# Gated recurrence on one core: a unit's opening moves from VectorE to ScalarE, and GpSimd's low terms are cut into six parts

## What is computed

```python
def hgrn2_chunk_scan(q, k, v, log_f):
    """Chunkwise S_t = diag(f_t) S_{t-1} + k_t v_t^T, o_t = S_t^T q_t, scanned in token order."""
    def step(state, inp):
        qb, kb, vb, fb = inp
        b = jnp.cumsum(fb, axis=2)
        diff = b[:, :, :, None, :] - b[:, :, None, :, :]
        decay = jnp.exp(jnp.where(scan_order[:, :, None], diff, -jnp.inf))
        scores = jnp.einsum('bhtd,bhtsd,bhsd->bhts', qb, decay, kb)
        o = jnp.einsum('bhts,bhse->bhte', scores, vb) + jnp.einsum('bhtd,bhde->bhte', qb * jnp.exp(b), state)
        b_last = b[..., -1]
        state = jnp.exp(b_last[:, :, 0, :, None]) * state + jnp.einsum('bhsd,bhse->bhde', kb * jnp.exp(b_last - b), vb)
        return state, o
```

## Time and profile before

| | us |
|---|---|
| median of 3 runs | 3597.81 |
| lowest, highest | 3596.05, 3600.88 |
| the profiled execution, whole | 3596.66 |
| its span, first to last instruction | 3594.8 |
| `stage_hgrn` in it, from the first sigmoid to the last `take` | 1984.8 to 2188.8 |

### The profile page before, as it was taken

The page is one execution under the profiler, slowest core; times in us unless marked ns, Lnnn a source line. Parts: engine busy times, 40 slices in busy tenths (PEclk is TensorE's granted clock), DMA queues, the critical chain, the costliest instruction groups (busy, mean ns, idle before and its releaser), DMA issues. The chain is left out here.

```text
span 3594.8 us, 42433 instructions
## 1 busy us (share of the span) xinstructions
PE 3327.1 (93%) x17158; PEld 2642.7 (74%) x17158; DVE 1702.4 (47%) x2635; ACT 1181.5 (33%) x1920; POOL 962.3 (27%) x412
## 2 busy tenths in 40 slices
PE   5999989988999799999999777989999888899998
PEld 4887667866888688888888664368887664578887
DVE  6995467554332323355510897552211585653211
ACT  3223364324443422122231224333222323543222
POOL 0001322432444122322332110024444221024443
PEclk7999999998999899999999998989999888899999
DMA  4222324451223222333321000012233110023332
GB/s 188 99 97 86 130 99 154 154 176 59 95 98 93 74 88 84 128 135 131 134 73 57 30 18 7 1 65 94 95 111 96 48 52 27 1 65 94 100 94 88
DMA packets 91790, 315.99 MB, mean 88 GB/s; under 512 B 10822, under 2 KB 12614, under 8 KB 90314
## 3 DMA queue, kind: packets, MB, share of 16 engines
q1 hardware_dynamic: 88876, 304.74, 25.8%
q10 hardware_dynamic: 2720, 8.55, 0.6%
HBM read 311.16 MB, written 2.10 MB: 87 GB/s over the span
## 5 line engine op out<-in xcount | busy, mean ns | idle before, releaser
L261 POOL TENSOR_TENSOR terms<-streams,terms 128x1024 fp32r<-128x1024 f32 (+2 forms) x408 | 962.1, 2358 | 2613.1 <-ACT terms L249 2613.1
L519 PE MATMUL bank<-terms,terms 128*128 128x512 f32 (+2 forms) x3776 | 1407.5, 373 | 24.2 <-POOL terms L261 10.3
L520 PE MATMUL bank<-terms,terms 128*128 128x512 f32 (+2 forms) x3776 | 1401.9, 371 | 0.0
L521 PE MATMUL bank<-terms,terms 128*128 128x512 f32 (+2 forms) x3776 | 1400.4, 371 | 0.0
L249 ACT ACTIVATE terms<-streams 128x1024 fp32r<-128x1024 f32 (+1 forms) x462 | 475.5, 1029 | 1741.6 <-PE bank L521 1494.0
L519 PEld LDWEIGHTS bank<-terms,terms 128*128 128x128 f32 x3776 | 715.5, 189 | 159.5 <-issue 30.9
L521 PEld LDWEIGHTS bank<-terms,terms 128*128 128x128 f32 x3776 | 715.0, 189 | 121.9
L520 PEld LDWEIGHTS bank<-terms,terms 128*128 128x128 f32 x3776 | 716.1, 190 | 119.1
L1946 DVE TENSOR_TENSOR stage<-stage,bank 128x256 f32<-128x256 f32 (+1 forms) x84 | 51.8, 618 | 544.4 <-ACT stage L1924 544.4
L1319 DVE SCALAR_TENSOR_TENSOR arena<-arena,vec 128x512 f32<-128x512 f32 x240 | 162.5, 745 | 0.2
L1910 DVE TENSOR_TENSOR terms<-stage,terms 128x512 fp32r<-128x512 f32 (+1 forms) x66 | 114.3, 1735 | 0.0
(11 more groups left out here) (379 smaller groups left out, 3476.8 us busy)
## 6 DMA issues: line engine op xcount, KB each, us to landing
streams<-in_ffn_w SPq DMA_DIRECT2D x104, 512.0 KB, 3.5
streams<-in_w_mod SPq DMA_DIRECT2D x72, 512.0 KB, 3.6
streams<-in_w_up SPq DMA_DIRECT2D x44, 512.0 KB, 3.5
streams<-in_w_gu SPq DMA_DIRECT2D x44, 512.0 KB, 3.5
streams<-in_w_ada SPq DMA_DIRECT2D x32, 512.0 KB, 3.5
streams<-in_w_down SPq DMA_DIRECT2D x32, 512.0 KB, 3.5
streams<-in_w_v SPq DMA_DIRECT2D x24, 512.0 KB, 3.7
streams<-in_ffn_w SPq DMA_DIRECT2D x24, 384.0 KB, 3.3
```

What stands on the lines that cost most here:

```text
L261: gp.tensor_tensor(self.low(m), self.raw(n), self.high(m), ALU.subtract).then_inc(self.low_made.sem, 1)
L519: pe.matmul(out, high[:, at], x_high, start=kk == start, stop=False)
L520: pe.matmul(out, high[:, at], x_low, start=False, stop=False)
L521: mm = pe.matmul(out, low[:, at], x_high, start=False, stop=kk == kts - 1)
```

## The change

Four things, all inside `stage_hgrn` and its helpers.

1. ScalarE's `gates(n)` does the whole opening of `pre` and `key`: two sigmoids and two Identity activations with scale and bias. A new `begin(n)` does what is left of the opening and of VectorE's level 1: it copies the key half (`x`, 128x256), copies half of `pre` into `suf` (128x384), and writes ones to the other half of `suf` (128x384). `begin(n + 1)` stands on ScalarE behind `place(n, 7)` and ahead of `keep(n)` and the two copies of the transposed keys, and waits for VectorE's last work on unit n.
2. VectorE drops L2295, L2296, L2297 and, at level 1, L2315 and L2320. It waits for `begun` before it updates `pre` at level 1.
3. `carry(n - 1)` moves from behind level 1 to behind level 2, `take(n - 1)` from level 3 to level 4, TensorE's `sums(n - 1)` from level 1 to level 3. `gates(n + 1)` waits for the states, not for `take`.
4. GpSimd makes the low term of unit n's tile in six parts of 170 or 171 columns during unit n+1, each part released by the VectorE instruction in front of a merge: the update of `pre` at level 1, the update of `suf` at levels 2 to 6. The last unit's tile is made whole, as before.

```diff
         @block.scalar
             def gates(n):
                 h, d = units[n]
-                act.activation(pres[n % 2], fpre[:, 2 * h + d, :], ACT.Sigmoid)
-                act.activation(keys[n % 2], fpre[:, 2 * h + d, :], ACT.Sigmoid, scale=-1.0).then_inc(gated.sem, 1)
+                pre, key, one = pres[n % 2], keys[n % 2], k.v("lb1", 4 * d + h)
+                act.activation(pre, fpre[:, 2 * h + d, :], ACT.Sigmoid).then_inc(opened.sem, 1)
+                act.activation(key, fpre[:, 2 * h + d, :], ACT.Sigmoid, scale=-1.0).then_inc(opened.sem, 1)
+                act.wait_ge(*opened(2 * n + 1))
+                act.activation(pre, pre, ACT.Identity, bias=k.v("lb0", 4 * d + h), scale=one)
+                act.wait_ge(*opened(2 * n + 2))
+                act.activation(key, key, ACT.Identity, scale=one).then_inc(gated.sem, 1)
+
+            def begin(n):
...
+                x, p4, s4, k4 = halves(both[1]), halves(pres[n % 2]), halves(suf), halves(keys[n % 2])
+                act.wait_ge(*gated(n + 1))
+                if n:
+                    act.wait_ge(*scored(8 * n))
+                    act.wait_ge(*ready(9 * n))
+                act.activation(x[:, :, kh], k4[:, CTX // 2:, kh], ACT.Copy).then_inc(begun.sem, 1)
+                act.activation(s4[:, :, kh], p4[:, :, qh], ACT.Copy).then_inc(begun.sem, 1)
+                act.activation(s4[:, :, qh], p4[:, :, qh], ACT.Identity, bias=1.0, scale=0.0).then_inc(begun.sem, 1)
...
                 if n + 1 < len(units):
                     if n:
-                        act.wait_ge(*taken(n))
+                        act.wait_ge(*states(n))
                     gates(n + 1)
                 place(n, levels - 1)
                 place(n, levels)
+                begin(n + 1)
                 inputs.keep(act, n)
                 act.wait_ge(*turned(n + 1))
...
         @block.vector
                 dve.wait_ge(*gated(n + 1))
-                dve.tensor_scalar(pre, pre, one, k.v("lb0", 4 * d + h), ALU.mult, ALU.add)
-                dve.memset(suf, 1.0)
-                link(dve.tensor_scalar(key, key, one, None, ALU.mult))
                 dve.sem_inc(ready.sem, 1)
...
+                    if lev == 1:
+                        dve.tensor_tensor(x[:, :, qh, :], q4[:, :, qh, :], p4[:, nctx:, qh, :], ALU.mult
+                                          ).then_inc(ready.sem, 1)
+                        dve.wait_ge(*ready(9 * n + 2))
+                        dve.wait_ge(*begun(3 * n + 3))
+                        link(dve.tensor_tensor(p4[:, :, qh, :], p4[:, :, qh, :], p4[:, :, kh, :], ALU.mult))
+                        if n >= 2:
+                            dve.wait_ge(*placed(2 * n - 2))
+                        merging[n].append(len(links))
+                        merge(n, 0)
+                        continue
...
                     if 1 < lev < levels:
+                        merging[n].append(at + 2)
                         merge(n, lev - 1)
...
-                    if lev == 1:
-                        if n:
-                            carry(n - 1)
-                        if n >= 2:
-                            dve.wait_ge(*placed(2 * n - 2))
-                        merge(n, 0)
-                    if n and lev == 3:
+                    if n and lev == 2:
+                        carry(n - 1)
+                    if n and lev == 4:
                         take(n - 1)
...
+    def low_beside(self, gp, n, merging):
+        d, i = self.tiles[n]
+        m = d.tiles[i][0][0] + PARTED
+        size = self.k.pieces[self.k.dense_at[m]][1]
+        cuts = [size * q // len(merging) for q in range(len(merging) + 1)]
+        for q, at in enumerate(merging):
+            gp.wait_ge(*self.k.dve_done(at))
+            self.k.make_low_part(gp, m, cuts[q], cuts[q + 1])
```

More of the change, by code:

```diff
@@ L153, in __init__ @@
         self.squared_early = sig("squared_early")
+        self.begun = sig("begun")
         self.ahead_high = sig("ahead_high")
@@ L261, in make_low, with make_low_part @@
         gp.tensor_tensor(self.low(m), self.raw(n), self.high(m), ALU.subtract).then_inc(self.low_made.sem, 1)
+    def make_low_part(self, gp, m, a, b):
+        if a == 0:
+            gp.wait_ge(self.high_made.sem, m + 1)
+            gp.wait_ge(self.piece_done.sem, m - PARTED + 1)
+        ins = gp.tensor_tensor(self.low(m)[:, a:b], self.raw(self.dense_at[m])[:, a:b], self.high(m)[:, a:b],
+                               ALU.subtract)
+        if b == self.pieces[self.dense_at[m]][1]:
+            ins.then_inc(self.low_made.sem, 1)
 def flat(ap):
@@ L2141, in stage_hgrn @@
     B = k.bank
-    tiled = k.more[11]
+    tiled, opened, begun = k.more[11], k.more[15], k.begun
     units = [(h, d) for h in range(HEADS2) for d in range(2)]
@@ L2160, in stage_hgrn @@
     k.act_done.counted(1)
-    links = []
+    links, merging = [], [[] for _ in units]
     def bank(n, lev):
@@ L2170, in _ @@
                 inputs.fetch(sp, n)
-        @block.gpsimd
-        def _(gp):
-            for n in range(len(units)):
-                inputs.low(gp, n)
         @block.scalar
@@ L2180, in gates, with halves @@
                 h, d = units[n]
-                act.activation(pres[n % 2], fpre[:, 2 * h + d, :], ACT.Sigmoid)
-                act.activation(keys[n % 2], fpre[:, 2 * h + d, :], ACT.Sigmoid, scale=-1.0).then_inc(gated.sem, 1)
+                pre, key, one = pres[n % 2], keys[n % 2], k.v("lb1", 4 * d + h)
[6 more added lines that the diff above has]
+            def begin(n):
+                if n >= len(units):
+                    return
+                h, d = units[n]
+                qh, kh = 1 - d, d
+                def halves(ap):
+                    return ap.rearrange("p (b s) -> p b s", s=2)
+                x, p4, s4, k4 = halves(both[1]), halves(pres[n % 2]), halves(suf), halves(keys[n % 2])
[6 more added lines that the diff above has]
+                act.activation(s4[:, :, qh], p4[:, :, qh], ACT.Identity, bias=1.0, scale=0.0).then_inc(begun.sem, 1)
             def place(n, lev):
@@ L2197, in _ @@
             gates(0)
+            begin(0)
             for n in range(len(units)):
@@ L2226, in _ @@
                     pe.wait_ge(*ready(9 * n + lev + 1))
+                    if lev == 1:
+                        pe.wait_ge(*begun(3 * n + 1))
                     if lev >= 3:
@@ L2239, in _ @@
                     inputs.multiply(pe, n, lev, tiled)
-                    if n and lev == 1:
+                    if n and lev == 3:
                         sums(n - 1)
@@ L2292, in _ @@
                 pre, key = pres[n % 2], keys[n % 2]
-                one = k.v("lb1", 4 * d + h)
                 dve.wait_ge(*gated(n + 1))
-                dve.tensor_scalar(pre, pre, one, k.v("lb0", 4 * d + h), ALU.mult, ALU.add)
-                dve.memset(suf, 1.0)
-                link(dve.tensor_scalar(key, key, one, None, ALU.mult))
                 dve.sem_inc(ready.sem, 1)
@@ L2343, in _ @@
             take(len(units) - 1)
+        @block.gpsimd
+        def _(gp):
+            for n in range(len(units)):
+                if n + 1 < len(units):
+                    inputs.low_beside(gp, n, merging[n + 1])
+                else:
+                    inputs.low(gp, n)
     n = len(units)
     for s, m in ((gated, n), (ready, 9 * n), (scored, 8 * n), (merged, 6 * n), (placed, 2 * n), (turned, n), (turn_copied, n),
-                 (kv_done, n), (states, n), (summed, n), (taken, n), (tiled, 2), (k.dve_done, len(links))):
+                 (kv_done, n), (states, n), (summed, n), (taken, n), (tiled, 2), (k.dve_done, len(links)),
+                 (opened, 2 * n), (begun, 3 * n)):
         s.counted(m)
```

## The result

The kernel before took 3596.93 us (median of 4 runs), the changed kernel **3615.66 us** (median of 4, 3611.13 to 3617.0). The ratio is **1.0049, 95% interval 1.0037 to 1.0062**: slower, by 18.7 us. The forecast was 3608 us, its range 3597 to 3617.

The account below looks back on a forecast made before the run. The prediction took VectorE's chain to bound stage_hgrn, with a wait for level 0 replacing its saved work. 3596.66 - 0.4 + 0.9 + 7.6 + 1 + 1 = 3606.8, median 1.15 above: 3608 us, range 3597 to 3617.

Parts of the forecast that it names:

- unit 0: First unit, opening without a unit before it: its first products start about 0.4 us earlier, -0.4 us.
- opening with the clock held: Openings of units 1 to 7: level 3 at t + 11.15 against t + 11.02, +0.13 us each, +0.9 us for seven.
- the clock in the openings: TensorE's clock falls in about nine of ten of seven openings, at 1.2 us each: +7.6 us, ends 0 and +12.
- clock and late levels elsewhere: Levels 1 and 2 late now and then, and TensorE's pause during the states: +1 us in all (0 to 3).
- GpSimd's parts: Low term in six parts: 0.03 us delay for five parts in seven units, +1 us, ends 0 and +5.
- rival 2: Merge and GpSimd block each other, holding back the next product 0.5 us: +17 us, 3624 with the rest; chance 0.12.
- Which chain sets the end: Openings: the first merge waits 4 us for TensorE's level 0, replacing VectorE's stall and work.
- the third rival: Faster: level 0 done early, merge starting by t + 5.0 to gain 7.2 us; about 3590; chance 0.13.
- ScalarE's chain: Openings: begin (1.1 us), keep and key copies sum to 3.52 us, state terms at t + 3.57 instead of t + 1.95.
- What a fall costs: Price of one clock fall in an opening: 1.2 us taken, at most 1.7 from 3.4 us at half speed.
- The second pause: TensorE's pause during the states can make the clock fall too; within +1 us in all (0 to 3).
- rival 1: The clock holds in the openings, supported by a 2.07 us gap at the stage's end: 3599.5, no change; chance 0.20.

Follow-up runs that it names:

- e1: The changed kernel with ScalarE's begin(n + 1) moved behind the copies of the transposed keys; median 3592.59 us, ratio 0.9997 to the kernel before.
- e3: The changed kernel with GpSimd's low term made whole again instead of in six parts; median 3613.14 us, ratio 1.0050 to the kernel before.
- e6: The changed kernel with carry, sums and take back at their old levels; median 3605.02 us, ratio 1.0011 to the kernel before.
- e7: The changed kernel with ten filling identity products in TensorE's gap behind the transposes; median 3607.73 us, ratio 1.0018 to the kernel before.
- e2: The changed kernel with 20 filling identity products in TensorE's gap behind the transposes; median 3617.26 us, ratio 1.0056 to the kernel before.
- e8: The changed kernel with begin(n + 1) behind the key copies and carry, sums, take at old levels; median 3586.62 us, ratio 0.9964 to the kernel before.
- e10: e6 with ten filling identity products in TensorE's gap behind the transposes; median 3593.0 us, ratio 0.9990 to the kernel before.
- e4: The kernel before with only the six parts of GpSimd's low term; median 3584.25 us, ratio 0.9969 to the kernel before.
- e5: e4 with the two scalings moved from VectorE to ScalarE's gates(n), no begin; median 3596.26 us, ratio 0.9974 to the kernel before.
- e9: e5 with four filling identity products in TensorE's gap between transposes and state terms; median 3579.94 us, ratio 0.9954 to the kernel before.
- e11: The kernel before with only four filling identity products in TensorE's gap between transposes and state terms; median 3596.78 us, ratio 1.0000.

## Why the prediction was right, and its term that was too small

The terms of the sum, in us of the profiled executions:

| term | predicted | measured | from |
|---|---|---|---|
| unit 0 | -0.4 | -0.7 | stage start to its last keys, 22.98 against 23.69, below |
| opening with the clock held | +0.9 | +1.7 | level 3 at t + 11.26 against 11.02, seven times |
| the clock in the openings | +7.6 | +14.7 | six times 13.71 - 11.26 |
| clock and late levels elsewhere | +1 | +1.5 | unit 1, below |
| GpSimd's parts | +1 | 0 | 2.34 us a level, as before |
| end of the stage | none | +2.8 | below |
| outside the stage | none | +0.3 | 1.15 ahead of it, -0.89 behind |
| sum | +10.1 | +20.3 | |

**The number lies in the range by luck.** The forecast's own range was 3602 to 3613, and 3615.66 lies above it. The stated range went on to 3617 to take in the lower part of rival 2, GpSimd against the merge, which the runs refute. The clock's term was given +12 as its end, and it came to +14.7; the units were forecast 25 to 26.5 us apart, and six of seven are 27.2 to 27.7. What the prediction had right is the mechanism; its largest term was too small by half.

**Which chain sets the end: right.** VectorE's work went, and in its place stands a wait with level 0 as its releaser, 4.18 us where the clock held (forecast: 4). e1 shows that it is this chain: with `begin` behind the copies the wait shrinks to 0.81 us. The point from which the third rival was to decide (merge before t + 5.0) lies on the right side too: e1's merges at t + 4.59 make the stage shorter than before.

**ScalarE's chain: right.** `begin` passed in 1.21 us (2062.15 to 2063.36; forecast 1.1, with a floor of 1.0 that its own 0.95 for 1,024 columns in `keep` didn't bear out), `keep` and the copies as in the sum, and the state terms started at t + 3.71 (forecast 3.57). The elements two apart cost no double: 384 columns follow each other by 0.44 us.

**Where the clock falls: right.** Nine of ten openings were forecast, six of seven had it, and so had all seven of e3 and of e6, which have the same gap.

**What a fall costs: the term that was mis-sized.** I took 1.2 us, with 1.7 as its end, from the 3.4 us at half speed of rows 8. The same rows 6 and 7 gave 2.25 us for work wholly at 1.2 GHz, and this is what came: 2.2 us. The low stretch began in the longer gap and lasted 6.8 us, so it held the state terms and level 0 entirely. The mistake was to carry the length of one low stretch over as a bound. The gap doesn't settle the length either: in e6, with the same gap of 2.7 us and more, three of seven low stretches are of 6.8 us and four of 3.4 (the window from 2112 to 2120 has a clock of 0.57, that from 2088 to 2094 one of 0.72). Where a 3.4 us stretch held the state terms, they took 2.93 us and level 0 1.20 to 1.27, together 1.5 us more, within the prediction's 1.7. Why the changed kernel has the long ones alone in its openings is open. With 2.2 in place of 1.2 the sum would have been 3596.66 - 0.4 + 0.9 + 7 x 0.9 x 2.2 + 1 + 1 = 3613, and 3614 for the median. e7 bears on the size from the other side: with the clock held in the openings, and all else late as it was, the seven units give back 7.8 us even with five later falls.

**The second pause: named, and about the right size.** It came in unit 1 alone. TensorE waited 1.93 us during the states, the windows from 2020 to 2024 have a clock of 0.56 and 0.59, and the take of the sums waited 1.51 us for products at half speed; the unit took 26.44 us instead of 24.7. In the units where the clock had fallen in the opening it did not fall again. e7 shows what that covered: once the openings are cured, five of seven units fall in the pause. There it is 1.94 to 2.02 us long, and the clock held behind two pauses of 2.02 us. So the one pause of rows 9, on which rival 1 leaned, couldn't show that such a pause is safe, and its reason, dense products before it, doesn't fit the trace: in the 4.4 us ahead of it TensorE did 0.88 us of transposes and 1.60 us of state terms.

**Unit 0: the sign right, the size in part luck.** Its first products start 5.42 us into the stage instead of 5.61, which is 0.2 us. In the seven other runs with this opening of unit 0 (e1, e2, e3, e6, e7, e8, e10) the unit is only 0.05 to 0.2 us shorter than before. The rest of the 0.7 us goes with the granted clock, which is low where the stage begins: it rose 9.0 us into the stage here and 10.3 us before (the windows from 1992 to 1994 have 0.77 and 0.73).

**The end of the stage: missed.** Behind the last unit there is no `begin`, the gaps are 0.92 and 0.96 us as they were, and the clock fell all the same; the state terms took 2.71 us and the first sums 0.77 us instead of 0.46. From the last keys to the final `take` it took 11.46 us against 8.63. The pair of gaps is the one after which it fell in unit 6 of the kernel before, so the risk was in the rows. Whether the change made it likelier here isn't shown. With the same gaps behind the last unit the clock fell with the state terms in e2, e3, e6 and e8 too, and not in e1, e4, e5, e7 and e10, nor in the kernel before; in e5 and e10 it fell some us later, and the last `take` ended 1.1 and 0.5 us later for it.

**GpSimd and the merge: the rival falls.** From the timeline of the changed kernel, unit 2:

```profile
2057.30 0.73 DVE L2298 COPY_PREDICATED sq<-masks,bank 128x512 f32<-128x512 uint8 x1
2057.46 0.55 POOL L270 TENSOR_TENSOR terms<-streams,terms 128x171 fp32r<-128x171 f32 x1 [1.79 <-DVE arena L2360]
...
2057.91 0.54 DVE L2368 TENSOR_TENSOR streams<-streams 128x384 f32<-128x384 f32 x1
```

The part runs wholly beside the merge (it ends at 2058.01, the merge at 2058.03). The merge has the length of rows 10, and the part that of the first one of an opening, which runs while VectorE waits (2065.01 above). It takes 0.55 us, not 0.62, and the product behind it, at its length of rows 10, isn't late. By the Trainium skill (SBUF — State Buffer, "SBUF: two separate sides") a VectorE instruction with at most one SBUF input, outside the two-port modes, doesn't contend with GpSimd for the shared pair of ports; this trace agrees for the merge, whose data is in PSUM and whose mask is in SBUF.

**The chances.** "Slower" had 0.52 and came. "Same" had as much as 0.38 because the clock's price was put at 1.2 us; at 2.2 us the forecast alone would have lain 16 us above the kernel before, over twice the bound.

## What to carry to other kernels

Work that is moved off the bounding engine has to be placed in the other engine's order by who waits behind it: three copies of 1.2 us in all made seven units 25 us longer where they stood ahead of two others that TensorE waits for. When a move leaves TensorE idle for longer than any gap that the profile shows, let the upper end of the price be all the work behind the gap at 1.2 GHz, and look whether anything independent (the states here) can be run in the wait that results. Try the parts of a bundle one by one: the least of them, six short GpSimd instructions in place of a long one, was worth more alone than the whole.

## What the runs showed that I had not expected

- **Low stretches of two lengths.** Before, in unit 6, 3.4 us at half speed; in the changed kernel's openings 6.8 us. e6 has both, and those of e1 and e7 have 3.4 us again (in e7: 0.78, 0.50 and 0.86 in the windows from 2020 to 2026, that is 0.88 + 2 + 0.56).
- **Cheap fillers.** With ten products or more in the gap of 2.7 us the granted clock stayed at 1.00 through all 21 openings (e2, e7, e10), also with 0.5 us of the gap left; without them it fell in 20 of 21 (the changed kernel, e3, e6). With four products in the gap of 0.96 us it stayed in all 16 (e9, e11, the last unit's keys counted in). Without them it fell in 12 of 46: one in the kernel before, none in e1, two each in e4 and e5, three in e8, and four of six behind last units elsewhere. The long gap is settled by this. For the short one it is a count over one profiled execution each, which speaks for the fillers but is no proof.
- **Falls move.** After an opening is cured, the next pause of 2 us in the unit becomes the place of the fall (e1, e2, e7), until that too has gone (e9, e10).
- **Stages that no edit touches scatter.** Executions of e5 differ by 21 us, and its profiled one lost 13.6 us behind the recurrence, at a lower granted clock there. What decides that is open. The stage's own time was the steadier reading: the rest of the program behind the stage was within 2 us in all profiled executions but those of e4 (1410.18) and e5.
